# The last down-projection step of each expert pair, multiplied expert by expert

## The reference

```python
def moe_ffn(x, router_w, router_bias, w_gate, w_up, w_down):
    ...                                   # 16 experts in 4 groups, 2 experts chosen per token
    hg = jnp.einsum('btd,edf->btef', x, w_gate)      # w_gate, w_up: 16 x 2048 x 512
    hu = jnp.einsum('btd,edf->btef', x, w_up)
    h = (jax.nn.silu(hg) * hu).astype(f32) * comb[..., None]
    return jnp.einsum('btef,efd->btd', h.astype(x.dtype), w_down)   # w_down: 16 x 512 x 2048
```

## Time and profile before

| | |
|---|---|
| median of three runs | 1753.64 us |
| the profiled execution | 1754.85 us, of it the span of the core 1753.1 us |
| PE busy | 1592.9 us, 91% of the span |
| DVE busy, ACT busy | 714.2 us, 466.4 us |
| DMA | 538.12 MB, 307 GB/s over the span |
| mean granted TensorE clock | 0.981 |
| down products, L1126 | 768 and 256 records |

### The profile page before, as it was taken

One profiled execution on the slowest core, in us unless ns is written; L12 is line 12 of the kernel. 1 busy time (PEld: TensorE's weight loads), 2 busy tenths in 40 slices (PEclk: granted clock), 3 DMA queues, 4 the chain that ended last, 5 costly groups with the idle time before them and its releaser, 6 DMA issues.

```text
span 1753.1 us, 18352 instructions
## 1 busy us (share of the span) xinstructions
PE 1592.9 (91%) x7223; PEld 944.2 (54%) x7223; DVE 714.2 (41%) x1217; ACT 466.4 (27%) x691; POOL 18.3 (1%) x38
## 2 busy tenths in 40 slices
PE   8999999997999889898879999999799988989875
PEld 7888887875533225333238788878543332533222
DVE  6675564656211112111157797656521112111116
ACT  5565445433110001000034345553220000100000
POOL 1000000000000000000000000000000000000000
PEclk9999999998999999999999999999899999999998
DMA  9666554783899999999994565538589999999995
GB/s 274 180 181 181 167 156 144 264 312 144 343 416 421 422 416 421 418 422 421 420 351 134 155 180 162 162 121 336 192 350 422 421 421 416 421 419 422 421 419 229
DMA packets 133541, 538.12 MB, mean 307 GB/s; under 512 B 19392, under 2 KB 20032, under 8 KB 87120
## 3 DMA queue, kind: packets, MB, share of 16 engines
q1 hardware_dynamic: 132880, 532.75, 79.9%
q0 software_dynamic: 576, 4.19, 0.7%
HBM read 534.82 MB, written 2.10 MB: 306 GB/s over the span
## 4 chain that ended last, share of the span: by engine, by line
PE 71%; DMA 20%; DVE 5%; issue 1%; ACT 1%; SPq 1%; POOL 0%; DVEq 0%
PE ps L1064 16%; PE ps L758 12%; PE ps L760 11%; PE ps L759 11%; DMA ring<-in_moe_w_down 10%; DMA ring<-in_moe_w_up 10%; PE ps L1126 9%; PE ps L1044 2%; PE ps L1045 2%; PE ps L739 2%; PE ps L1053 1%; SPq L604 1%; PE ps L1054 1%; PE ps L1243 1%; PE ps L1257 1%
## 5 line engine op out<-in xcount | busy, mean ns | idle before, releaser
L758 PE MATMUL ps<-w_lo,x_hi 128*128 128x512 f32 x880 | 350.3, 398 | 7.0 <-DVE x_lo L2357 1.8
L759 PE MATMUL ps<-w_hi,x_hi 128*128 128x512 f32 x880 | 344.5, 391 | 0.0
L1808 DVE TENSOR_TENSOR w_lo<-ring,w_hi 128x1024 fp32r<-128x1024 f32 x224 | 270.3, 1222 | 181.7 <-ACT w_hi L1350 180.2
L1350 ACT ACTIVATE w_hi<-ring 128x1024 fp32r<-128x1024 f32 x224 | 235.8, 1059 | 309.2 <-PE ps L760 303.5
L2251 DVE TENSOR_TENSOR arena<-ps,arena 128x512 f32<-128x512 f32 x120 | 77.6, 686 | 418.9 <-PE ps L1054 418.9
L758 PEld LDWEIGHTS ps<-w_lo,x_hi 128*128 128x128 f32 x880 | 166.3, 189 | 46.4 <-issue 7.6
L759 PEld LDWEIGHTS ps<-w_hi,x_hi 128*128 128x128 f32 x880 | 166.2, 189 | 34.5 <-issue 0.5
L1064 PE MATMUL ps<-arena,hT 128*64 128x512 f32 x768 | 173.0, 605 | 8.0 <-DVE hT L2241 4.3
L1126 PE MATMUL ps<-ring,arena 128*64 128x512 f32 x768 | 172.2, 599 | 7.4 <-DMA ring<-in_moe_w_down 7.4
L760 PE MATMUL ps<-w_hi,h_lo 128*128 128x512 f32 x384 | 150.2, 391 | 0.0
L1562 ACT ACTIVATE y_hi<-ps 128x512 fp32r<-128x512 f32 x60 | 33.9, 596 | 435.3 <-PE ps L1126 220.4
(11 more groups left out here) (337 smaller groups left out, 1531.7 us busy)
## 6 DMA issues: line engine op xcount, KB each, us to landing
arena<-in_moe_w_gate SPq DMA_DIRECT2D x48, 2048.0 KB, 19.6
ring<-in_moe_w_down SPq DMA_DIRECT2D x96, 1024.0 KB, 18.2
arena<-in_moe_w_up SPq DMA_DIRECT2D x32, 2048.0 KB, 21.3
ring<-in_moe_w_up SPq DMA_DIRECT2D x32, 2048.0 KB, 21.5
ring<-in_ab_w_in SPq DMA_DIRECT2D x96, 512.0 KB, 3.7
ring<-in_moe_w_gate SPq DMA_DIRECT2D x16, 2048.0 KB, 21.4
arena<-in_moe_w_down SPq DMA_DIRECT2D x32, 1024.0 KB, 18.3
ring<-in_c_w_in SPq DMA_DIRECT2D x64, 512.0 KB, 3.7
```

The source lines that it names most:

```text
L758: nc.tensor.matmul(t, x_h, w_l[:, k, :], start=(opens and k == 0), stop=False)
L759: nc.tensor.matmul(t, x_h, w_h[:, k, :], start=False, stop=False)
L1350: act.activation(high_unit(n), raw_unit(n)[0], ACT.Copy).then_inc(w_hi_ready, 1)
L1808: v.tensor_tensor(lo, raw, high_unit(n).bitcast(FP32), ALU.subtract).then_inc(w_lo_ready, 1)
```

## The change

Each layer gets one more semaphore, `end_loaded`. The first DMA of step 11 (expert 0) adds to it; all other DMAs of that slot, the second DMA of step 11 among them, add to `loaded[5]` as before, and the counts waited for are changed to fit. PE no longer waits for both DMAs ahead of step 11: it waits for `end_loaded`, does expert 0's four matmuls, waits for `loaded[5]`, and does expert 1's four. The other steps keep their wait and their order. DMAs, sizes, matmuls and `step_used` stay as they are.

```diff
                 if not (first and i == 0):
                         pe.wait_ge(s["y_ready"], 4 * x)
                     for st in range(8, STEPS):
-                        pe.wait_ge(s["loaded"][st % 6], 48 * x + 48)
+                        if st < STEPS - 1:
+                            pe.wait_ge(s["loaded"][st % 6], 48 * x + 48)
...
-                        for jj in range(w.shape[2]):
-                            j = rows + jj
-                            for c in range(w.shape[3] // BANK):
-                                for e in range(2):
-                                    last = nc.tensor.matmul(ps[2 + 2 * half + c][e * CAP:(e + 1) * CAP, :], hT_e[:, j, e * CAP:(e + 1) * CAP],
-                                                            w[:, e, jj, c * BANK:(c + 1) * BANK], start=(j == 0), stop=(j == 3),
-                                                            skip_group_check=True)
+                        for e in range(2) if st == STEPS - 1 else ((0, 1),):
+                            if st == STEPS - 1:
+                                if e == 0:
+                                    pe.wait_ge(s["end_loaded"], 16 * x + 16)
+                                else:
+                                    pe.wait_ge(s["loaded"][st % 6], 32 * x + 32)
+                            for jj in range(w.shape[2]):
+                                j = rows + jj
+                                for c in range(w.shape[3] // BANK):
+                                    for e_ in (e,) if st == STEPS - 1 else e:
+                                        last = nc.tensor.matmul(ps[2 + 2 * half + c][e_ * CAP:(e_ + 1) * CAP, :],
+                                                                hT_e[:, j, e_ * CAP:(e_ + 1) * CAP], w[:, e_, jj, c * BANK:(c + 1) * BANK],
+                                                                start=(j == 0), stop=(j == 3), skip_group_check=True)
                         last.then_inc(s["step_used"], 1)
...
-                    sp.dma_start(to, w).then_inc(loaded, 16)
+                    sp.dma_start(to, w).then_inc(M[lay]["end_loaded"] if st == STEPS - 1 and n == 0 else loaded, 16)
...
-                    pe.wait_ge(s["loaded"][st % 6], 48 * x + 16 if 2 <= st < 6 else 16 * (2 * x + st // 6 + 1))
+                    pe.wait_ge(s["loaded"][st % 6], (32 if st == 5 else 48) * x + 16 if 2 <= st < 6 else 16 * (2 * x + st // 6 + 1))
```

More of the change, by code:

```diff
@@ L421, in program @@
             s = {name: sem(f"{name}_{lay}") for name in (
-                "step_used", "silu_ready", "pT_full", "pT_ready", "h_ready", "hT_full", "hT_ready",
+                "step_used", "end_loaded", "silu_ready", "pT_full", "pT_ready", "h_ready", "hT_full", "hT_ready",
                 "y_hi_ready", "y_ready", "comb_ready", "pick_ready", "ln_ready", "h_hi_ready", "h_lo_ready", "acc_ready")}
```

## The result

The changed kernel takes 1763.1 us (median of five runs, 1761.1 to 1764.7) against 1753.7 us: 9.4 us more, a ratio of 1.0051 (95% interval 1.0036 to 1.0066). 1760.9 us was predicted, with a range of 1752.6 to 1768.5. The profiled execution took 1764.7 us, its span is 1762.9 us.

The account below looks back on a forecast made before the run. Weight loads were taken to bound the experts' stage, with PE's last step counting at layer ends and short-queue places. Per layer 2.6 + 0.7 + 0.4 = 3.7 us, 7.3 for two, added to 1753.64: 1760.9 us, range 1752.6 to 1768.5.

Parts of the forecast that it names:

- What bounds the kernel: Experts' stage: weight loads set the pace, so a longer last step counts only at layer ends and where the load queue is short.
- The count of slots: Last step: one waiting pass can be overtaken, so 14 slots of 0.43 us instead of 8, 2.6 us more.
- The router's row: Profile row for the router: four matmuls in four quarters, eight passes, take 0.64 us, not more than two passes alone.
- My alternative of three waiting places: Last step, three waiting places per half: 4 added slots, 3.4 us in all; a partial form of the overlap rival, chance 0.32.
- The end of a layer: Last step before ACT's copy at each layer's end: it stands in the chain, so its full 2.6 us is lost.
- Pair 1, reserve 2.7 us: Pair 1 of a layer: PE 2.6 us later, covered by 2.7 us of queued loads, so 0 lost.
- Pairs 4 and 5: Second group: lags of 2.6 and 5.2 us against reserves of 1.9 and 4.1 us lose 0.7 and 0.4 us a layer.
- a rate of 328 GB/s: Transfer rate in the profile before, dipping for a microsecond at pair 4's low point of the load queue, reserve 1.9 us.
- a rival about the half-used array: Last steps: half-used array lowers the granted clock, 8.5 us more per step, over 20 us a layer, above 1790 us; chance 0.03.
- 5.2 + 2.1 = 7.3 us: Both layers' sum: 2.6 us at each layer's end, plus losses in pairs 4 and 5 of 1.1 us a layer.
- What it gains: Expert 0's early start at a layer's end: worth nothing, as PE is busy with the scatter until both halves have landed.
- The added wait: One more instruction per pair in PE's sequencer, 16 in all: 0.1 us a layer at most, left out.

Follow-up runs that it names:

- blocks of two, three and four: Kernel before, last step's products alternating between experts in rows of two (1754.3 us), three (1756.1 us) or four per expert (1762.7 us).
- the filler runs: Unused products added where PE waits for DVE and ACT: changed kernel 1757.8 us, ratio 1.0017; kernel before 1752.7 us, ratio 0.9990.

## Why the prediction was right, and where it was right by luck

- What bounds the kernel: right. The last step counts in two places; new order in pairs 1, 2, 5 and 6 costs 0.5 us, within nothing.
- The count of slots: the mechanism was right, the term mis-sized. I took one waiting pass as what may be overtaken, "the trace needs that one and no more", and 14 slots. Three may be, and the step has 12: 1.76 us, not 2.6. The router's row, four matmuls in four quarters, had shown three overtaken, and I set it aside because they are in different parts of the array. A bound on the total, wherever they wait, fits that row and these runs; no run tells it from a bound per part. My alternative of three waiting places gave exactly the 4 slots, but 3.4 us in all as its sum.
- The end of a layer: right in kind, 1.76 us each, 3.5 us in all (measured 3.5 with the order changed there alone) for 5.2 predicted.
- Pair 1, reserve 2.7 us: nothing was lost, as predicted. The stretch from 425 to 530 us ran at 337 GB/s after and 334 before.
- Pairs 4 and 5: this is the step that failed. I had 1.1 us a layer for a lag of 2.6 and 5.2 us, and by the same reserves a lag of 1.76 and 3.5 us would have cost nothing. Measured: 5.3 us for both layers with the ends left alone. Two things were missing. The reserve read from the landings is not a clean threshold: with the clock up and steps 1.76 us longer the window still loses 1.4 us more than before. The earlier trace rows had the sign of it, a rate of 328 GB/s in a place where I counted 1.9 us in hand. And the clock falls there in some executions, which delays PE by 1.46 us in one step (5.11 for 3.65), on top of the lag. I had read the clock's rows, but used them for a rival about the half-used array. Its price, over 20 us a layer (14 x 0.85 - 3.6 is 8.3 us a step, not 8.5), did not come, and the fall comes with both halves at work as well.
- So 5.2 + 2.1 = 7.3 us was predicted, and 3.5 + 5.3 to 5.9 = 8.8 to 9.4 measured: one term too large by 1.7, one too small by 3.2 to 3.8. That the sum came within 2.2 us is partly luck: with the right count of slots the same reserves give 3.4 us, about 1757.
- What it gains: right, nothing. The order alone costs as much as the change.
- The added wait: right, nothing.
- The Trainium skill's page "TensorE: Matmul & The Clock Gate" (Part 3, "The mechanism") has matmuls start in strict program order; the runs with blocks of two, three and four contradict it for matmuls in different column halves: in the blocks of three expert 1's first pass starts ahead of three of expert 0's. "TensorEngine Tiling (Array Packing)" (Key Properties), tiles operate independently, holds only for what lies within three waiting passes. The first page's section "Why this matters for your kernels" advises against long gaps between bursts of matmuls in which PE is idle. The waits here, 1.6 and 0.9 us, are shorter than those it warns of, so the filler runs, with 4.7 us of loss in place of 8.9, agree with it in kind only.

## What to carry to other kernels

Two matmuls in different column halves are free for each other only if they stand close together in the program: alternate them, or keep rows of one half to two float32 matmuls. Before an operation is moved ahead of a wait, look whether the engine could have started earlier at all in the place that is in the chain; here it was busy with a scatter until after the second transfer had landed. A reserve read from the profile is shared: a small lag that it should cover can cost several microseconds, in part because a fall of the clock draws on the same reserve.

## What the hardware showed that I had not expected

- A pass overtook at most three waiting ones: rows of 4, 6 and 8 passes of one half took 8, 10 and 12 slots (3.65, 4.51 and 5.37 us).
- The granted clock falls to its lower level for some microseconds behind waits of 1.6 and 0.9 us in one execution and not in another with the same waits: at 720 to 724 us it was 1.00 before, 0.67 after and 0.58 with the old order and both semaphores. Filler products of 0.4 to 1.7 us in such waits kept it at 1.00 through pairs 4 and 5, and made the kernel before 1.7 us faster (ratio 0.9990, 0.9980 to 0.9999). That is the fastest version of this study, faster than both kernels, the kernel before by little more than the interval allows.
